# The first token tile in falling order: one stationary per head for a level's keys, level differences on POOL

## What is computed

```
f = lb + (1 - lb) * sigmoid(f_logit);  k = 1 - f;  q = silu(q)
b = cumsum(log f) within chunks of 64 tokens
a[t, s] = sum_d q[t,d] k[s,d] exp(b[t,d] - b[s,d])     for s <= t in the chunk
o = a @ i  +  (q exp(b)) @ state                        state carried from chunk to chunk
```

```
gp = pad(gate, 2 tokens in front);  h = conv_b + sum_j gp[t + j] * conv_w[j]   (3 taps)
```

## Time and profile before

| | |
|---|---|
| runs | 1106.81, 1106.96, 1107.94 us |
| the profiled execution | 1107.21 us, of which its span 1105.1 us |
| PE / DVE / ACT / POOL busy | 99% / 64% / 53% / 3% of the span |
| granted TensorE clock | 0.999 over the span, 1.00 in each stretch cited |
| the level steps | 529.8 us (level 0 of the first half) to 656.8 us (level 128 of the second) |
| DMA, HBM | 180 GB/s over the span |

### The profile page before, as it was taken

The page is one execution under the profiler, slowest core; times in us unless marked ns, Lnnn a source line. Parts: engine busy times, 40 slices in busy tenths (PEclk is TensorE's granted clock), DMA queues, the critical chain, the costliest instruction groups (busy, mean ns, idle before and its releaser), DMA issues.

```text
span 1105.1 us, 13962 instructions
## 1 busy us (share of the span) xinstructions
PE 1094.9 (99%) x5660; PEld 931.0 (84%) x5660; DVE 708.4 (64%) x830; ACT 586.3 (53%) x775; POOL 38.3 (3%) x49
## 2 busy tenths in 40 slices
PE   9999999999999999999999999999999999999997
PEld 7888999988888888888888888888888888888886
DVE  6567676754685655567986778657647555756552
ACT  6473655443476544467654546553356556656341
POOL 2800000000000000000000000010000000000000
PEclk9999999999999999999999999999999999999999
DMA  9855655555676555474443434457456336555541
GB/s 362 287 176 166 224 175 178 187 190 191 213 224 185 183 183 182 144 266 155 151 153 115 152 129 141 151 205 252 161 174 218 114 115 207 179 187 189 191 152 39
DMA packets 126271, 200.17 MB, mean 181 GB/s; under 512 B 6400, under 2 KB 74160, under 8 KB 126080
## 3 DMA queue, kind: packets, MB, share of 16 engines
q1 hardware_dynamic: 122848, 187.72, 50.5%
q0 software_dynamic: 3216, 11.51, 3.1%
q10 hardware_dynamic: 144, 0.07, 0.0%
HBM read 198.22 MB, written 1.05 MB: 180 GB/s over the span
## 4 chain that ended last, share of the span: by engine, by line
PE 91%; DVE 4%; ACT 2%; issue 1%; DMA 1%; SPq 0%; DVEq 0%; ACTq 0%
PE ps L598 19%; PE ps L600 19%; PE ps L599 19%; PE ps L637 4%; PE ps L635 4%; PE ps L636 4%; PE ps L734 3%; PE ps L910 3%; PE ps L912 3%; PE ps L911 3%; PE ps L981 2%; DVE rest L1708 1%; ACT high L1196 1%; PE ps L1130 1%; PE ps L1115 1%
## 5 line engine op out<-in xcount | busy, mean ns | idle before, releaser
L1708 DVE TENSOR_TENSOR rest<-raw,high 128x2048 fp32r<-128x2048 f32 x131 | 302.2, 2325 | 123.6 <-ACT high L1196 123.4
L598 PE MATMUL ps<-high,xt_high 128*128 128x512 f32 x728 | 289.4, 398 | 0.0
L600 PE MATMUL ps<-high,xt_rest 128*128 128x512 f32 x728 | 284.1, 390 | 0.0
L599 PE MATMUL ps<-rest,xt_high 128*128 128x512 f32 x728 | 283.6, 390 | 0.0
L1196 ACT ACTIVATE high<-raw 128x2048 fp32r<-128x2048 f32 x131 | 247.4, 1913 | 61.8 <-DMA raw<-in_ffn_w_down_dram 22.3
L600 PEld LDWEIGHTS ps<-high,xt_rest 128*128 128x128 f32 x728 | 136.6, 188 | 29.1
L599 PEld LDWEIGHTS ps<-rest,xt_high 128*128 128x128 f32 x728 | 136.9, 188 | 26.8
L598 PEld LDWEIGHTS ps<-high,xt_high 128*128 128x128 f32 x728 | 136.8, 188 | 26.6
L1713 DVE SCALAR_TENSOR_TENSOR rest<-raw,wgain,high 128x512 fp32r<-128x512 f32 x176 | 119.1, 746 | 50.3 <-ACT high L1200 50.3
L1200 ACT ACTIVATE high<-raw,wgain 128x512 fp32r<-128x512 f32 x176 | 110.9, 720 | 9.6 <-DMA raw<-in_ffn_w_in_dram 9.6
L910 PE MATMUL ps<-xt_high,high 128*128 128x256 f32 x288 | 81.7, 284 | 0.0
(11 more groups left out here) (336 smaller groups left out, 1484.9 us busy)
## 6 DMA issues: line engine op xcount, KB each, us to landing
raw<-in_w_in_dram SPq DMA_DIRECT2D x88, 512.0 KB, 4.2
raw<-in_ffn_w_in_dram SPq DMA_DIRECT2D x88, 512.0 KB, 4.7
raw<-in_w_up_dram SPq DMA_DIRECT2D x44, 512.0 KB, 4.6
raw<-in_ffn_w_down_dram SPq DMA_DIRECT2D x44, 512.0 KB, 4.0
raw<-in_w_down_dram SPq DMA_DIRECT2D x22, 512.0 KB, 4.4
raw<-in_w_out_dram SPq DMA_DIRECT2D x16, 512.0 KB, 4.6
raw<-in_w_mkv_dram SPq DMA_DIRECT2D x16, 512.0 KB, 4.8
raw<-in_w_branch_a_dram SPq DMA_DIRECT2D x8, 512.0 KB, 4.2
```

The source lines that it names most:

```text
L598: pe.matmul(out, sh, wh, start=first, stop=False)
L599: pe.matmul(out, sh, wr, start=False, stop=False)
L600: mm = pe.matmul(out, sr, wh, start=False, stop=last)
L1708: vec.tensor_tensor(rest[:, slot, c], raw[:, slot, c], high[:, slot, c].bitcast(F32), ALU.subtract).then_inc(unit_rest, 1)
```

## The change

- x is laid out on the host with tokens 0 to 127 reversed, and the output's order is restored there; constants that depend on the position (rope, decay, window, the causal mask, now one for each tile) follow.
- In the recurrence the tiles change places in the buffers and the layout becomes half, tile, head, position. In the rising tile a block's keys are its first half, in the falling one its second. So the keys of both tiles fill one stationary of 128 columns for a head, and the queries of both its 128 moving columns. A level is four matmuls of 128 columns instead of eight of 64; products across tiles are masked out. The masks take 1144 columns (1024 before).
- `diff` moves from DVE to POOL. All 16 differences stand in POOL's queue before the load of `mem` and of gain `mem_kv`, behind a wait on `hb_ready`; each waits on `level_ready`.
- The running sums of the falling tile can't be scanned forward: for each half of the heads two scans of 512 elements stand for four of 256, then come a sum over 8 elements, a copy of 8 and an addition of 8x63 elements, each waiting for the one before. The attention's gate sums take two scans of 128, a copy of 1, and two instructions over 128.
- Each tap of the convolution has its columns at the tile's edge in instructions of one column: six more per block.
- One more small load (`starts`) stands in POOL's queue with the masks.

```
+            def diff(n):                                   # in POOL's queue
+                hf, lv = HG_STEPS[n]
+                pool.wait_ge(sem("level_ready"), n)
+                if lv == 128:
+                    ...  (a sum of 128x4, a wait on it, three pieces of 128x256)
+                else:
+                    ...
+                        ins = pool.tensor_tensor(every(e, HALF * P), every(b, HALF * P), ref, ALU.subtract)
+                ins.then_inc(sem("level_diff"), 1)
...
             for n, name in enumerate(GAINS):
+                if name == "mem_kv":
+                    pool.wait_ge(sem("hb_ready"), 2)
+                    for k, (_, lv) in enumerate(HG_STEPS):
+                        if lv:
+                            diff(k)
...
                     for h in range(HALF):
-                        for tt in range(TT):
-                            ...
-                            mm = pe.matmul(out[0:P - lv, c:c + P // 2], hqk[:, h, keys], q, start=True, stop=True)
+                        mm = pe.matmul(grid(out, h * CHUNK, (S, TT), (1, CHUNK)), hqk[:, 0, h * P:(h + 1) * P],
+                                       grid(hqk[:, 1, :], h * CHUNK, (S, TT), (1, CHUNK)), start=True, stop=True)
...
-                        d = conv[:, j % 2, c, back:S]
-                        ins = vec.scalar_tensor_tensor(d, src[:, c, 0:S - back], ...)
+                        for m in range(back):
+                            first = d[:, P + m:P + m + 1]
+                            step(vec.scalar_tensor_tensor(first, g[:, back - 1 - m:back - m], w, first, ALU.mult, ALU.add))
+                        d = grid(d, 0, (P + back, TT), (1, P - back))
+                        ins = vec.scalar_tensor_tensor(d, grid(g, back, (P - back, TT), (1, P - back)), w, d, ALU.mult, ALU.add)
...
-                    elif n + 1 < len(HG_STEPS) and HG_STEPS[n + 1][1]:
-                        diff(n + 1)                        # in DVE's slot, behind apply_decays(n)
...
-                    took(("flog", 1), vec.tensor_tensor_scan(fcum[:, :], fones[:, :], src, 0.0, ALU.mult, ALU.add))
+                    step(vec.tensor_tensor_scan(fcum[:, 0:P], fones[:, 0:P], src[:, 0:P], 0.0, ALU.mult, ALU.subtract))
+                    step(vec.tensor_tensor_scan(fcum[:, P:S], fones[:, P:S], src[:, P:S], 0.0, ALU.mult, ALU.add))
+                    settle()
+                    step(vec.tensor_copy(fones[:, 0:1], fcum[:, P - 1:P]))
+                    settle()
+                    step(vec.tensor_scalar(fcum[:, P:S], fcum[:, P:S], fones[:, 0:1], None, ALU.subtract))
+                    took(("flog", 1), vec.scalar_tensor_tensor(fcum[:, 0:P], fcum[:, 0:P], fones[:, 0:1], src[:, 0:P],
+                                                               ALU.subtract, ALU.add))
...
-                    for h in range(HALF * k, HALF * k + HALF):
-                        step(vec.tensor_tensor_scan(hb[:, h, :], scanstart[:, :], hb[:, h, :], 0.0, ALU.mult, ALU.add))
+                    step(vec.tensor_tensor_scan(flat(hb[:, k, 0, :, :]), scanstart[:, :], flat(he[:, 0, :, :]), 0.0, ALU.mult, ALU.add))
+                    b, l, total = by_chunk(hb[:, k, 1, :, :]), by_chunk(he[:, 1, :, :]), hqk[:, 0, 0:rows]
+                    step(vec.tensor_tensor_scan(flat(hb[:, k, 1, :, :])[:, 1:last + 1], scanstart[:, 0:last], flat(he[:, 1, :, :])[:, 0:last],
+                                                0.0, ALU.mult, ALU.subtract))
                     settle()
+                    step(vec.tensor_tensor(total, l[:, :, CHUNK - 1], b[:, :, CHUNK - 1], ALU.subtract))
+                    settle()
+                    step(vec.tensor_copy(b[:, :, 0], total))
+                    settle()
+                    vec.tensor_tensor(b[:, :, 1:CHUNK], b[:, :, 1:CHUNK], total.unsqueeze(2).to_broadcast([P, rows, CHUNK - 1]), ALU.add)\
+                        .then_inc(sem("hb_ready"), 1)
+                    vec.wait_ge(sem("hb_ready"), k + 1)
```

More of the change, by code:

```diff
@@ L60, with grid, key_tokens, query_tokens @@
 LEVELS = (1, 2, 4, 8, 16, 32, 64)
+MASK_AT = {0: 0}
+MASKS = P
+for _lv in LEVELS:
+    MASK_AT[_lv] = MASKS
+    MASKS += TT * HALF * (P // (2 * _lv))
+ORDER = np.concatenate([np.arange(P)[::-1], np.arange(P, S)])
+def grid(ap, at, *dims):
+    return bass.AP(ap.tensor, ap.offset + at, (tuple(ap.ap[0]),) + dims)
+def key_tokens(ap, width, lv):
+    return grid(ap, 0, (width + lv, TT), (2 * lv, HALF * P // (2 * lv)), (1, lv))
+def query_tokens(ap, width, lv):
+    return grid(ap, lv, (width - lv, TT), (2 * lv, HALF * P // (2 * lv)), (1, lv))
 NEG = -1e30
@@ L260, in build @@
         ident, identb, causal = small["ident"], small["identb"], small["causal"]
-        levelmask, scanstart = small["levelmask"], small["starts"]
+        levelmask = small["levelmask"]
         sums, roots, recips = small["sums"], small["roots"], small["recips"]
@@ L561, in _ @@
             rotate(0, rq)
-            for name, src in (("wgain", "ffn_pre"), ("convw", "conv_w"), ("convb", "conv_b"), ("causal", "c_causal"), ("starts", "c_starts")):
+            for name, src in (("wgain", "ffn_pre"), ("convw", "conv_w"), ("convb", "conv_b"), ("causal", "c_causal")):
                 pool.dma_start(small[name][:], dram[src]).then_inc(consts1_landed, 16)
@@ L1057, in _ @@
                                    [stage[:, (j - 1) % 2, tt, c * P:(c + 1) * P]
-                                    for c in (2 * g, 2 * g + 1) for tt in range(TT)])
+                                    for c in (2 * g, 2 * g + 1) for tt in tiles])
                 for n in HG_SLOT[u]:
@@ L2369, in constants @@
     f32 = np.float32
-    tok = np.arange(S)
+    tok = ORDER
     out = {"c_ident": np.eye(P, dtype=f32), "c_identb": np.eye(P, dtype=f32).astype(np.dtype("bfloat16"))}
-    causal = np.where(np.arange(P)[None, :] <= np.arange(P)[:, None], 0.0, NEG).astype(f32)
-    out["c_causal"] = causal.astype(np.dtype("bfloat16"))
-    starts = np.broadcast_to((tok % CHUNK != 0).astype(f32), (P, S))
+    at = tok.reshape(TT, P)
+    causal = np.where(at[None, :, :] <= at.T[:, :, None], 0.0, NEG).astype(f32)
+    out["c_causal"] = np.ascontiguousarray(causal).astype(np.dtype("bfloat16"))
+    starts = np.broadcast_to((np.arange(HALF * P) % CHUNK != 0).astype(f32), (P, HALF * P))
     out["c_starts"] = np.ascontiguousarray(starts).astype(np.dtype("bfloat16"))
```

174 lines of the change are left out of this document (89 added, 85 removed).

## The result

| | before | after |
|---|---|---|
| median of the runs | 1106.96 us | 1101.30 us (five runs, 1101.02 to 1102.64) |
| span of the profiled execution | 1105.1 us | 1099.5 us |
| ratio | 1 | 0.9946, 95% interval 0.9935 to 0.9956 |

The changed kernel is 0.54% faster. The forecast was 1108.9 us, slower by 0.2%; the direction was wrong.

A forecast was written before the change was run, and what follows sets the result against it. PE, busy 99% of the span, bounds the kernel, with DVE and ACT setting the front of the recurrence. First half +3.4, second -1.5, sum +1.9 us: median 1108.9 us, range 1100 to 1114 us.

The forecast's parts named there:

- What the differences on POOL cost: Recurrence slots: a difference costs POOL 2.39 us, in series with DVE's products and `rest`; DVE is freed of 1.23 us.
- the line of 7.4 and 7.15 us sets the pace: First half: with no reserve at its start, DVE and POOL in series set the slots instead of PE's 6.3 us.
- PE's 4.35 us are eaten: First half: level 128 comes 3.4 us late (3.1 to 3.8), so PE's saving there is lost.
- The sum of the line: Recurrence slot: products, difference, `rest` and waits add to 7.4 us if `rest` goes first, 6.9 if POOL does.
- PE's saving: Recurrence, 14 groups of score matmuls: 0.62 us saved in each, 8.7 us in all, 4.35 per half (bounds 8.2 and 9.2).
- Level 128: End of each half: PE waits 3 us there for POOL's three pieces of 128x256 at 0.72 us and what follows.
- The front: Before level 1 of the first half: scans, gate sums and first difference delay it 2.8 us (bounds 0.5 and 4).
- The serial line itself: Recurrence: POOL's difference, DVE's `rest` and products exclude each other for whole instructions and the two orders take turns.
- Rival 1: Recurrence: PE keeps its saving, POOL's work finds gaps beside masked copies and ACT; -6.4 us, 1100.6 us, chance 0.25.
- Rivals 2 and 3: Recurrence: POOL's difference dearer than its addition, 1114 us, chance 0.18; all masked copies cost 1.3 us, 1112 us, chance 0.07.
- The convolution: Its 66 one-column instructions, 11 us of DVE, are covered by DVE's waiting: 0, or 1 us with a tenth uncovered.
- Larger masks and moved loads: POOL's queue before the recurrence and loads behind the last difference: larger masks, one more load and moved loads cost 0.

The follow-up runs named there:

- Experiment 5: Changed kernel with POOL's differences of levels 1 to 64 reading two different tiles in the first half, one tile in place in the second; 1104.33 us, ratio 0.9971.
- experiment 3: Changed kernel with all 16 differences back on DVE at their old places, none on POOL; 1100.42 us, ratio 0.994.
- experiment 4: Changed kernel with only levels 1 and 2 of the first half differenced on POOL, the other 14 back on DVE; 1098.72 us, ratio 0.9925.
- experiment 2: Kernel before with only the differences moved to POOL, matmuls and sums as before; 1105.99 us, ratio 0.9987.
- experiment 9: Changed kernel without the three dependent steps behind the second scan of the gates; 1099.76 us, ratio 0.9927.
- experiment 7: Changed kernel with the attention's gate sums as one scan again, falling tile's sums left out; 1100.30 us, ratio 0.9936.
- experiment 10: Changed kernel without the convolution's 66 one-column instructions; 1101.74 us, ratio 0.9945.
- experiment 1: Changed kernel with POOL's differences, except level 128, subtracting a full-size tensor (hb from itself) instead of the repeated reference; 1101.12 us, ratio 0.9946.

## Why the prediction was wrong, point by point

- **The step that failed** is the price in "What the differences on POOL cost": "POOL's addition of 128x1024 took 2.39 us; that is my price for a difference". It came from an addition of two different tensors; the difference reads one tensor and a repeated element of it, and takes 1.9 us. Experiment 5 puts 2.4 us of the first half's error on it (47.77 against 45.34), the largest single part. No row of before showed such a difference on POOL, and the forecast kept no bound below its price: it had only a rival in which the difference is dearer. The price alone does not carry the direction: with it in the first half the kernel still takes 0.9971 of the time before. What followed from it, "the line of 7.4 and 7.15 us sets the pace" and "PE's 4.35 us are eaten", needed the two errors below as well.
- **The sum of the line** (7.4 and 6.9 us) was 0.2 too long in each slot even at that price (experiment 5: 7.17 and 6.69), because durations that overlap were added end to end; that cause is read from the trace and was not tested by itself. With level 128's part it makes 1.6 us over the first half. With both errors the line no longer sets the pace of the first half: 6.47 and 6.67 us are what PE needs with its new scores (6.34 in the plain slots of experiments 3 and 4) and 0.1 to 0.3 more, which the view of the waits does not list.
- **PE's saving** was right in kind and too small: 8.7 us forecast, with bounds 8.2 and 9.2; 10.2 shown, 5.1 in experiment 3's second half and as much in experiment 4's first (busy 43.00 us, 48.19 before). From L981 at 546.96 to the next unit's first matmul at 548.74 a group held PE 1.78 us before and holds it 0.91 now (547.49 to 548.40). The forecast took one group's 1.52 from spacings between starts of records averaged over all levels and did not read the start of what follows. Its own figures disagree there: a slot of 7.14 us "of which the unit is 5.4" leaves 1.74 for the group, and 6.3 after the change means 0.84 saved, not 0.62. The page's 8.4 us is less than 10.2, because PE waits between records in the changed kernel's slots (busy 43.58 and 43.66 us where experiment 4 has 43.00 and 43.50) and was busy 0.8 us longer in the first 100 us, before any of this.
- **Level 128** waits 1.6 and 1.0 us, not 3. The pieces of 128x256 take 0.61 us each when alone (experiment 2), not 0.72; L557, the source of the price, reads two different tensors (`stage` and `ropes`). In the changed kernel the first of them stands beside a `rest` (2.72 us); that order was foreseen.
- **The front** had 2.8 us (bounds 0.5 and 4) and got 1.6. The same instructions of DVE in three traces divide it. Before:

```profile
524.84 1.34 DVE L2234 MEMSET ha<- 128x1536 f32 x1 [0.39 <-DVE hb L2202]
529.58 2.29 DVE L1708 TENSOR_TENSOR rest<-raw,high 128x2048 fp32r<-128x2048 f32 x1
```

  In experiment 3 the `rest` behind the gate sums:

```profile
531.62 2.29 DVE L1758 TENSOR_TENSOR rest<-raw,high 128x2048 fp32r<-128x2048 f32 x1
```

  In the changed kernel:

```profile
526.10 1.34 DVE L2291 MEMSET ha<- 128x1536 f32 x1 [0.39 <-DVE hb L2258]
532.33 2.29 DVE L1759 TENSOR_TENSOR rest<-raw,high 128x2048 fp32r<-128x2048 f32 x1
```

  The scans' steps cost 1.3 us up to the clearing of `ha`, where 1.9 stood (experiment 9 has 1.5). The gate sums cost another 0.8 up to `rest` in experiment 3, where 0.85 stood. POOL's first difference adds 0.7 in the changed kernel (L2200: 0.98 against 0.28), where 1.2 had been set aside; of the 1.1 us of experiment 7 a part is this. The difference was ready beside a `rest`, as said, but then it lay beside scans from PSUM, the cheap one of the two cases between which the middle was taken. With the first difference gone from DVE (-1.1, forecast -1.15) these make the measured 1.6.
- **The serial line itself held**: `rest` at 3.92 beside POOL, POOL at 3.88 beside `rest`, turn and turn about. Rival 1 gave 1100.6 us and was nearest to the 1101.3, but not for its reason: POOL's work found no gaps beside DVE's `rest`. The time is near because the line, in series, is about as short as PE's need. That the result lies inside the range of 1100 to 1114 us is owed to this rival's end of it.
- **Rivals 2 and 3** are refuted: the difference is cheaper than the addition, and the masked copies of levels 4 to 64 take 0.71 to 0.75 us.
- **The convolution** at no cost was right (experiment 10). Larger masks and moved loads left no wait in the trace.
- **In sum**: forecast +1.9 us, the three stretches of the profile -5.8, a gap of 7.7. The front holds 1.2 of it, the first half 4.0 (2.4 price, 1.6 the rest of the line and level 128; PE's larger saving counts there only as far as it lets the shorter line through). The second half holds 2.5: PE's larger saving, 0.75, and the shorter wait at level 128. How far that second wait is price and how far overlap was not separated.

## What to carry to other kernels

Price a moved instruction from one with the same shape and the same kind of operands (two different tensors, or one and a repeated element of it), and where there is none keep both signs of the difference as bounds; here 0.5 us in 2.4, in the first half alone, was worth 2.8 us of the whole (experiment 5, ratio 0.9971 against 0.9946), half of what the change gains. When an engine's work is moved to one that excludes it, the sum doesn't shrink: move only what stands in a slot that the first engine bounds (two of sixteen differences here), and let it start when the other's long instruction has ended. Where two orders of pieces differ by 0.2 us from a third engine's need, read the start-to-start times of the pieces, not their durations.

## What the runs showed of the hardware

- **POOL's two-input operation has two prices, by what its inputs are.** 128x1024 in f32: 1.89 to 2.02 us when the second input is a repeated element of the first one's tensor or the same addresses once more (the changed kernel, experiments 1 and 5), and 2.38 to 2.42 with two different tensors (experiment 5 and the rotation); 128x256: 0.61 against 0.72. That the inputs lie in two tiles is not enough by itself: with a repeated element of another tile 128x256 takes 0.61 too (experiment 2). Two different full inputs of one tile were not run, so whether the number of elements read or the distance of their addresses decides is open. The Trainium skill has one price for this operation (page "GPSIMD Engine Reference", section 3.1, 4497 ns at 2048 elements). Half of that is 2.25 us, an estimate; the runs here lie on both sides of it.
- **The exclusion can reach a short instruction of one input.** L2200, `tensor_scalar` of 40x128 in SBUF, took 0.98 us beside POOL's difference and 0.28 without it. The scans that read PSUM took 0.39 and 0.40 in both, and a copy of 40x1 in SBUF took 0.15 us beside the difference.
- **The masked copy's time depends on the level.** On levels 1 and 2 it takes 1.31 and 1.32 us, on the others 0.71 to 0.75, at the same 128x512 now that all levels have the same shape. Before it was the same with 127 and 126 partitions, and since the mask's operand changed with the layout and the time did not, the mask's pattern of single and double elements is the likely cause; it was not tested.
